# New distances between activation buffers and weight buffers, and a later place for the decay matrices

## What is computed

```python
n1 = rmsnorm(h, norm1_g); q, k, v, r, a_lr, su, sv, ga, gb = split(n1 @ w_in)
h = h + (sigmoid(ga) * (gla(q, k, v, r, a_lr) @ w_branch_a)
         + sigmoid(gb) * (sgu(su, sv) @ w_branch_b)) @ w_out
h = rmsnorm(h + peer(rmsnorm(h)))      # 8 heads, top 16 of 128 x 128 experts

# second block, x = h and a context of 256 tokens, both modulated by c
x, ctx = x + 0.5 * g1 * swiglu(mod(x)), ctx + 0.5 * g1c * swiglu(mod(ctx))
# retention, 4 heads: decay matrices exp(lg * distance), forward and backward
sc = einsum('hid,hjd->hij', qc, kc) * decay
o = einsum('hij,hjv->hiv', sc, vc)
x = x + g2 * (merge(retention, fourier) @ w_out)
x = rmsnorm(x + 0.5 * g3 * swiglu(mod(x)))
```

## Time and profile before

| | us |
|---|---|
| median of three runs | 2139.4 |
| lowest and highest | 2136.89, 2142.93 |
| profiled execution | 2133.73 |
| its span, first to last instruction | 2131.9 |
| TensorE busy in the span | 2085.4 |
| VectorE, ScalarE busy | 1229.2, 1037.7 |

### The profile page before, as it was taken

The page is one execution under the profiler, slowest core; times in us unless marked ns, Lnnn a source line. Parts: engine busy times, 40 slices in busy tenths (PEclk is TensorE's granted clock), DMA queues, the critical chain, the costliest instruction groups (busy, mean ns, idle before and its releaser), DMA issues.

```text
span 2131.9 us, 35635 instructions
## 1 busy us (share of the span) xinstructions
PE 2085.4 (98%) x12718; PEld 1822.9 (86%) x12718; DVE 1229.2 (58%) x2082; ACT 1037.7 (49%) x1585; POOL 143.2 (7%) x82
## 2 busy tenths in 40 slices
PE   8999999999999999999999999999999999999998
PEld 6899999778888888888888888887888898899997
DVE  5457795996666666666665333323655644356554
ACT  5645644775555555555553222213444444336664
POOL 1001677000000000000000000000000000000000
PEclk9999999999999999999999999999999999999999
DMA  5435565886555555565543222322233245254563
GB/s 202 156 123 178 185 214 183 287 307 210 194 187 188 187 189 185 190 204 193 184 154 119 96 92 92 112 92 83 96 103 118 95 151 179 89 188 139 178 203 130
DMA packets 95668, 343.97 MB, mean 161 GB/s; under 512 B 11010, under 2 KB 11522, under 8 KB 95332
## 3 DMA queue, kind: packets, MB, share of 16 engines
q1 hardware_dynamic: 94196, 337.02, 47.1%
q0 software_dynamic: 1248, 5.57, 0.7%
q10 hardware_dynamic: 144, 0.26, 0.0%
HBM read 341.76 MB, written 1.05 MB: 161 GB/s over the span
## 4 chain that ended last, share of the span: by engine, by line
PE 88%; issue 6%; DVE 4%; ACT 2%; POOL 1%; DMA 0%; SPq 0%; ACTq 0%; DVEq 0%; POOLq 0%
PE ps L1656 16%; PE ps L1658 15%; PE ps L1657 15%; PE ps L1920 8%; PE ps L1934 6%; PE ps L1936 6%; PE ps L1935 5%; PE ps L1922 4%; PE ps L1689 2%; PE ps L1690 2%; PE ps L1691 2%; DVE TMP L1013 1%; PE ps L2165 1%; PE ps L2166 1%; PE ps L2167 1%
## 5 line engine op out<-in xcount | busy, mean ns | idle before, releaser
L993 DVE TENSOR_TENSOR WL<-RAW,WH 128x1024 fp32r<-128x1024 f32 x517 | 625.1, 1224 | 408.5 <-ACT WH L510 402.5
L510 ACT ACTIVATE WH<-RAW 128x1024 fp32r<-128x1024 f32 x565 | 585.3, 1053 | 240.3 <-PE ps L1936 106.7
L1656 PE MATMUL ps<-XH,WH 128*128 128x256 f32 (+1 forms) x1200 | 382.5, 319 | 6.0 <-DVE XL L1022 3.7
L1657 PE MATMUL ps<-XL,WH 128*128 128x256 f32 (+1 forms) x1200 | 379.1, 316 | 0.0
L1658 PE MATMUL ps<-XH,WL 128*128 128x256 f32 (+1 forms) x1200 | 379.1, 316 | 0.0
L1920 PE MATMUL ps<-XHL,WH 128*128 128x512 f32 x752 | 268.6, 397 | 0.0
L1656 PEld LDWEIGHTS ps<-XH,WH 128*128 128x128 f32 x1200 | 229.1, 191 | 24.4 <-DVE XL L1022 4.3
L1657 PEld LDWEIGHTS ps<-XL,WH 128*128 128x128 f32 x1200 | 229.3, 191 | 14.6
L1658 PEld LDWEIGHTS ps<-XH,WL 128*128 128x128 f32 x1200 | 229.2, 191 | 14.4
L1922 PE MATMUL ps<-XHL,WL 128*128 128x256 f32 x752 | 210.9, 280 | 0.0
L1934 PE MATMUL ps<-WH,AH 128*128 128x512 f32 x512 | 202.4, 395 | 0.0
(11 more groups left out here) (340 smaller groups left out, 3354.1 us busy)
## 6 DMA issues: line engine op xcount, KB each, us to landing
RAW<-in_wstream SPq DMA_DIRECT2D x625, 512.0 KB, 3.3
ADB<-in_wstream SPq DMA_DIRECT2D x12, 512.0 KB, 4.8
H<-in_xT SPq DMA_DIRECT2D x4, 256.0 KB, 6.4
CTX<-in_ctxT POOLq DMA_DIRECT2D x1, 1024.0 KB, 7.9
HX<-in_ctxT POOLq DMA_DIRECT2D x1, 1024.0 KB, 5.9
DIST<-in_dist POOLq DMA_DIRECT2D x1, 1024.0 KB, 6.3
out<-Y SPq DMA_DIRECT2D x3, 256.0 KB, 2.6
MASK<-in_mask POOLq DMA_DIRECT2D x1, 512.0 KB, 4.0
```

Source lines behind the costliest of these rows:

```text
L510: act.activation(WH[:, slot, :], RAW[:, slot, :], ACT.Copy).then_inc(hi_ready, 1)
L993: dve.tensor_tensor(WL[:, slot, :], RAW[:, slot, :], WH[:, slot, :].bitcast(F32), ALU.subtract).then_inc(lo_ready, 1)
L1656: pe.matmul(dst, wh, xh, start=start, stop=False, skip_group_check=not check)
L1657: pe.matmul(dst, wh, xl, start=False, stop=False, skip_group_check=not check)
```

## The change

H and XHL move by 96 bytes, so XHL lies 96 bytes from the grid. AH and AL, 32 bytes behind XHL's new end, lie at 128. REG starts 32 bytes behind them, at 160, and with it all tiles that are placed from it (XRA, XH2, HIDH, YRH, YFH, G and others). XRP gets 224 bytes more and so lies at 64 instead of 192. MH gets 352 more and lies at 512. HX, IDENT2 and the tiles behind them follow by 96. RAW, WH, WL and DIST stay. Every instruction keeps its shape and count.

In the heads the two Exps of the decay matrices, with their wait, move from the head's start to behind the split of chunk 8 of the head (`j == 6`), in the middle of the value chunks, and VectorE's wait, masks and sum move behind the splits `j` = 5 to 7, ahead of VL.

```diff
--- before.py
+++ after.py
@@ -176,14 +176,14 @@
         RAW = sb("RAW", [P, 4, 1024], 0)
         WH = sb("WH", [P, 4, 1024], dt=F32R)
         WL = sb("WL", [P, 4, 1024], dt=F32R)
-        H = sb("H", [P, KB, T])
+        H = sb("H", [P, KB, T], 49152 + 96)
         XHL = sb("XHL", [P, 2, KB, T], dt=F32R)
         XH, XL = XHL[:, 0, :, :], XHL[:, 1, :, :]
-        AHP = place[0]
-        AH = sb("AH", [P, 2, T], dt=F32R)
+        AHP = place[0] + 32
+        AH = sb("AH", [P, 2, T], AHP, dt=F32R)
         AL = sb("AL", [P, 2, T], dt=F32R)
-        REG = place[0]
-        G = sb("G", [P, NKEYS, T])
+        REG = place[0] + 32
+        G = sb("G", [P, NKEYS, T], REG)
         CL = sb("CL", [P, NCOLS])
         MOD = sb("MOD", [P, MODB, 2])
         SCG = sb("SCG", [P, 3, KB, 2])
@@ -224,13 +224,13 @@
         MV = sb("MV", [P, TT, 2])
         TMPM = sb("TMPM", [P, 2, T])
         MG = sb("MG", [P, KB, T])
-        XRP = sb("XRP", [P, 2, KB, T], dt=F32R)
+        XRP = sb("XRP", [P, 2, KB, T], place[0] + 224, dt=F32R)
         KEEP = REG + 131072 - 8192
         assert place[0] <= KEEP
         K12T = sb("K12T", [P, 2, P], KEEP)
         QT = sb("QT", [P, 4, T])
         assert place[0] <= REG + 131072
-        MH = sb("MH", [P, KB, T], REG + 28672, dt=F32R)
+        MH = sb("MH", [P, KB, T], REG + 28672 + 352, dt=F32R)
         ML = sb("ML", [P, KB, T], dt=F32R)
 
         XRA = sb("XRA", [P, 2, KB, T], REG, dt=F32R)
@@ -265,7 +265,7 @@
         assert place[0] <= REG
 
 
-        HX = sb("HX", [P, KB, 2 * T], 57344)
+        HX = sb("HX", [P, KB, 2 * T], 57344 + 96)
         XH2 = sb("XH2", [P, KB * 2 * T], REG, dt=F32R)
         XL2 = sb("XL2", [P, KB * 2 * T], dt=F32R)
         R2 = place[0]
@@ -314,7 +314,7 @@
         MG2 = sb("MG2", [P, KB, T], R3)
         TMP2 = sb("TMP2", [P, 2, T])
         DIST = sb("DIST", [P, 2, 4, T], 49152)
-        IDENT2 = sb("IDENT2", [P, P], 73728)
+        IDENT2 = sb("IDENT2", [P, P], 73728 + 96)
         OST6 = sb("OST6", [P, TT, 6])
         OMV = sb("OMV", [P, TT, 2])
         SSUM = sb("SSUM", [P, TT, 2])
@@ -867,10 +867,6 @@
             HC = C0["heads"]
             act.wait_ge(s["tables_landed"], 64)
             with act.Fori(0, RH) as it:
-
-                act.wait_ge(s["p_ready"], it + 1)
-                act.activation(EF[:, :, :], DIST[:, 0, :, :], ACT.Exp, scale=LGD[:, 3, bass.ds(it, 1)]).then_inc(s["decay_exp"], 1)
-                act.activation(EB[:, :, :], DIST[:, 1, :, :], ACT.Exp, scale=LGD[:, 3, bass.ds(it + RH, 1)]).then_inc(s["decay_exp"], 1)
                 for j in range(2, 4):
                     split_hi(HC + j + 2, it, 12)
 
@@ -884,6 +880,10 @@
                 act.activation(KH[:, :, :], KR[:, :, :], ACT.Copy).then_inc(s["qk_hi"], 1)
                 for j in range(5, 8):
                     split_hi(HC + j + 2, it, 12)
+                    if j == 6:
+                        act.wait_ge(s["p_ready"], it + 1)
+                        act.activation(EF[:, :, :], DIST[:, 0, :, :], ACT.Exp, scale=LGD[:, 3, bass.ds(it, 1)]).then_inc(s["decay_exp"], 1)
+                        act.activation(EB[:, :, :], DIST[:, 1, :, :], ACT.Exp, scale=LGD[:, 3, bass.ds(it + RH, 1)]).then_inc(s["decay_exp"], 1)
                 act.wait_ge(chunk_done, at(HC + 8, 12, it))
                 act.activation(VH[:, :, :], ps[:, 4:8, :], ACT.Copy).then_inc(s["v_hi"], 1)
                 for j in range(8, 10):
@@ -1478,11 +1478,6 @@
                 dve.sem_inc(s[name], 1)
             with dve.Fori(0, RH) as it:
                 step.begin(it, 7)
-
-                dve.wait_ge(s["decay_exp"], at(2, 2, it))
-                dve.tensor_tensor(EF[:, 0:2, :], EF[:, 0:2, :], MASK[:, 0, :, :], ALU.mult)
-                step.link(dve.tensor_tensor(EB[:, 0:2, :], EB[:, 0:2, :], MASK[:, 1, :, :], ALU.mult))
-                step.link(dve.tensor_tensor(EF[:, :, :], EF[:, :, :], EB[:, :, :], ALU.add))
                 for j in range(2, 4):
                     split_lo(HC + j + 2, it, 12)
 
@@ -1504,6 +1499,11 @@
                 dve.tensor_tensor(KL[:, :, :], KR[:, :, :], KH[:, :, :].bitcast(F32), ALU.subtract).then_inc(s["qk_lo"], 1)
                 for j in range(5, 8):
                     split_lo(HC + j + 2, it, 12)
+
+                dve.wait_ge(s["decay_exp"], at(2, 2, it))
+                dve.tensor_tensor(EF[:, 0:2, :], EF[:, 0:2, :], MASK[:, 0, :, :], ALU.mult)
+                step.link(dve.tensor_tensor(EB[:, 0:2, :], EB[:, 0:2, :], MASK[:, 1, :, :], ALU.mult))
+                step.link(dve.tensor_tensor(EF[:, :, :], EF[:, :, :], EB[:, :, :], ALU.add))
                 dve.wait_ge(s["v_hi"], at(1, 1, it))
                 dve.tensor_tensor(VL[:, :, :], ps[:, 4:8, :], VH[:, :, :].bitcast(F32),
                                   ALU.subtract).then_inc(s["v_lo"], 1)
```

## The result

The changed kernel takes 2146.7 us (median of 8 executions, 2142.6 to 2147.8), the kernel before 2138.0 us in 8 beside them: a ratio of 1.0034 (95% interval 1.0022 to 1.0046). By that ratio it is 7.3 us slower. The forecast was 64 us faster.

The account below looks back on a forecast made before the run. TensorE was taken as the bound, its matmul intervals depending on operand addresses. Savings of 38.6 + 11.5 + 8.6 + 5.4 = 64.1 us gave 2075 us for the median, own range 2020 to 2120 us, with 2020 to 2125 as the stated range.

Parts of the forecast that it names:

- What bounds the kernel: Whole kernel: TensorE, busy 98% of the span; each matmul costs its columns plus 13.3 ns, which depend on operand addresses.
- Rival A: All stages: the address does not matter and only the decay matrices' 5.4 us remain, 2134 us; chance 0.09.
- The 7152: On-grid fp32r matmuls (4776 of 256 columns, 2376 of 512): 5.4 ns saved each at 96 or 160 bytes, 38.6 us.
- Rival B: The 7152 matmuls: new distances settle in a worse state, 5.8 ns more each, 2175 us in all; chance 0.05.
- The expert loop: 752 wide and narrow pairs save 15.4 ns each, 11.5 us; 1536 down matmuls save half of 11.2 ns, 8.6 us.
- XRP: Its 384 matmuls, moved from 192 to 64 bytes: 2 us either way, taken as 0.
- Decay matrices: Head 0: moving them later removes a 3.8 us TensorE wait and 1.5 us at half clock, 5.4 us saved.
- The sum: Whole kernel: 38.6 + 11.5 + 8.6 + 5.4 = 64.1 us saved.
- C: Rival: another engine or the transfers take over in the expert loop, whose 20 us go, 2095 us; chance 0.04.

Follow-up runs that it names:

- m1: A kernel of its own without the computation: four matmul forms at 18 operand distances, only TensorE working; 256 columns took 113.3 to 120.0 ns, 512 took 226.7 to 234.4.
- e2: The kernel before with the new addresses, decay matrices left at their old place; 1.0062 (1.0045 to 1.0079) of the kernel before.
- e1: The kernel before with only the decay matrices moved later, all addresses as before; 0.9969 (0.9958 to 0.9981) of the kernel before.
- e3: The changed kernel with REG and all in it back at distance 0; 0.9984 (0.9970 to 0.9997) of the kernel before.
- v2: v1 with H, XHL and HX at 160 bytes instead of 192; 0.9880 (0.9860 to 0.9901) of the kernel before.
- v1: The kernel before with late decay matrices, 192 bytes where 256 columns move, 0 for first-layer XH2, HIDH and AH; 0.9872 of the kernel before.
- m3: A kernel without the computation, high and low activation parts at 8 x 8 distances; 113.3 ns only at (192, 192), 226.7 only at (0, 0).

## Why the prediction was wrong

**What bounds the kernel** was right: TensorE, read by starts. That the 13.3 ns above the columns are a matter of addresses was right too. Rival A, that they are not, falls with m1 and with e2, whose addresses alone cost 13.3 us.

**"The 7152" is the step that failed.** They were to give 38.6 us and in sum cost about 10 (up 7.1, down 4.0 and 1.6, heads 1.8, less 2.7, 1.5 and 0.4, against e1). The mechanism, the place of one operand against the other, was right; the size and for 512 columns the sign were wrong. The term took the value of one form at one distance, XRP's 256 columns at 192, and gave 5.4 ns to 256 and 512 columns at 96 and 160. The opening had prepared this: from 120.0 and 226.7 it concluded that each matmul costs "its columns and 13.3 ns more, whatever its size", which holds at distance 0 alone. In m1 the price above the columns (106.7 and 213.3 ns) at 160 is 11.9 ns for 256 and 21.1 ns for 512. So:

- 256 columns (4776, expected -25.8 us): XHL at 96 stays at 120.0. The 1.1 us that `pre` takes more than in e1 are no matter of intervals: TensorE waits once, 1.10 us, for a WL of GpSimd, and e3, with XHL at the same place, has 104.3 us. At 160 the projections and the last layer gain 1.5 and 2.7 us. The nearest row was the luckiest one: in m1 113.3 appears at one distance of eight.
- 512 columns (2376, expected -12.8 us): up 7.1 us and down 4.0 us more in the first layer, 1.6 us more in the last down; the 480 in the heads and the Fourier branch, at 233.3 ns, cost 3.2 us, and their stage 1.8 in sum. Here there was nothing to win: distance 0 was the best.

The bounds allowed savings alone (2 to 10 ns), though no row showed either distance, nor 512 columns off the grid; the expert loop stood there as a stage that is worse than 226.7. Rival B was the right mechanism, with a chance of 0.05 and a place too wide: it put all 7152 in a worse state, but only the 512-column part went there (7.9 ns more in the first layer, where B had 5.8).

**The expert loop.** Pairs were to fall by 15.4 ns and fell by 1.2 (351.2 to 350.0); down matmuls were to fall by 5.6, half of 11.2, and rose by 1.4 in the loop (231.9 to 233.3). The term counted 1536 down matmuls at 232.5, while 420 of them stand outside the loop, 384 of these at 226.7 already; at 128 they lost 5.7 ns. Pairs and down matmuls were to give 20.1 us (20.2 by the prediction's own factors) and brought a loss of 3 to 4.

**XRP** was right in size: the stage went from 57.5 to 57.3 us. The two kinds became one, 117.8 ns in 15 of 16 chunks; the other one has 113.3.

**Decay matrices** were right: 5.4 us forecast, 6.6 (4.1 to 9.0) measured by e1, 5.5 in the traces (3.8 of the norms' stage, 1.7 of the heads'). The cover held: VH still waits up to 8.5 us.

**The sum**, read anew against e1: up 7.1, down 4.0 and 1.6, experts 4.0, heads 1.8, `pre` 1.1, less 2.7, 1.5, 0.4 (second output) and 0.2 (`wq`) makes 14.8 us lost. The modulation stage was 1.9 us shorter, within what it varies by between executions of any addresses: 12.9, beside 12.8 us between the spans. Of C only the one wait of 1.1 us in `pre` was seen.

What stays open: how the place of one operand against the other comes to cost time, what the period of 256 bytes stands for, and what decides the state that a run of matmuls enters. The runs show that states exist, last and change at interruptions, not why. Which forms and distances have them is not settled either: more than one was seen with 256 columns at 64, 160 and 192 and with the activation stationary at 192, while the up stage of the first layer took 253.0 us in every kernel at 0, and 260.1 us in both at 160. No kernel was profiled often enough to say how often a state comes.

## What to carry to other kernels

A stall that depends on addresses is measured for each shape and each distance before anything is moved by it; one stage at one distance says nothing of the next. The sweep that settles this costs one small kernel with TensorE alone. Swept with its own order of matmuls, it foretold a turn of the real loop within 0.01 us and the stages that v2 changed within 1 us; for the whole of v1 it promised 34 us and 27 came, and part of the gap are runs that entered the dearer state, as MH and blocks of the features did. If the 256- and the 512-column stages want different places, the region's base is the wrong handle: give each tile its own distance.

## What the runs showed of the hardware

With fp32r operands the start-to-start time at full clock hangs on the distance of the moving from the stationary operand, modulo 256 bytes: 113.3 to 120.0 ns with 256 columns, 226.7 to 234.4 with 512, with no other engine at work (m1). Where high and low part differ, 121.1 and 235.6 are reached (m3). Both operands moved by 160 bytes together keep 226.7 (the products of PTH and VH). The same addresses can settle in different states: with 256 columns 113.3 or 117.8 ns at 192 and 117.4 or 120.0 at 160, with the activation stationary 228.9 or 233.3 at 192. A state holds until the run of matmuls is interrupted, for over 40 chunks in the last layer, and is worth up to 4.5 us there from one execution to the next; in `wq` the states alternate from chunk to chunk.
